# Gates and projections of a gated block, computed with tokens as the stationary operand

## The reference

```python
def hybrid_layer(x, norm_g, w_in, q_norm_g, k_norm_g, sgu_norm_g, w_s, b_s, w_proj_a, w_proj_b, w_out):
    h = rms_norm(x, norm_g)
    q, k, v, z_a, u_b, v_b, z_b, g_a, g_b = jnp.split(h @ w_in, cuts, axis=-1)   # 7 x 1024, 2 x 2048
    ...
    att = moba_attention(q, k, v)                       # 8 heads, 256 tokens: plain causal softmax
    y_a = (att * jax.nn.silu(z_a)) @ w_proj_a           # 1024 -> 2048
    sgu = spatial_gating(jax.nn.gelu(u_b), jax.nn.gelu(v_b), sgu_norm_g, w_s, b_s)
    y_b = (sgu * jax.nn.silu(z_b)) @ w_proj_b           # 1024 -> 2048
    merged = jax.nn.sigmoid(g_a) * y_a + jax.nn.sigmoid(g_b) * y_b
    return x + merged @ w_out
```

## Time and profile before

| | us |
|---|---|
| median of 3 runs | 1817.54 (1817.28 to 1817.78) |
| profiled execution | 1817.34 |
| its span, first to last instruction | 1815.6 |
| TensorE busy | 1805.1 (99%) |
| VectorE busy | 1164.2 (64%) |
| ScalarE busy | 825.0 (45%) |
| weights | 624 transfers of 512 KB |

### The profile page before, as it was taken

The page is one execution under the profiler, slowest core; times in us unless marked ns, Lnnn a source line. Parts: engine busy times, 40 slices in busy tenths (PEclk is TensorE's granted clock), DMA queues, the critical chain, the costliest instruction groups (busy, mean ns, idle before and its releaser), DMA issues.

```text
span 1815.6 us, 28929 instructions
## 1 busy us (share of the span) xinstructions
PE 1805.1 (99%) x9540; PEld 1547.3 (85%) x9540; DVE 1164.2 (64%) x1521; ACT 825.0 (45%) x1116; POOL 129.0 (7%) x163
## 2 busy tenths in 40 slices
PE   9999999999999999999999999999999999999999
PEld 7888888878888888888888887888899888888987
DVE  5457777556755665576456656755687766668844
ACT  6334444446443443344334445744444454444542
POOL 1012323000000000000000000100013010100000
PEclk9999999999999999999999999999999999999999
DMA  7565555555566556556655565565565555555554
GB/s 252 190 222 165 163 169 162 182 177 185 180 218 194 179 187 199 187 185 192 192 192 184 188 194 178 190 204 194 179 192 173 185 175 170 167 171 185 185 190 158
DMA packets 93618, 337.50 MB, mean 186 GB/s; under 512 B 10864, under 2 KB 11008, under 8 KB 93184
## 3 DMA queue, kind: packets, MB, share of 16 engines
q1 hardware_dynamic: 92096, 331.39, 56.6%
q0 software_dynamic: 752, 5.26, 0.8%
q10 hardware_dynamic: 720, 0.17, 0.0%
HBM read 334.67 MB, written 2.11 MB: 185 GB/s over the span
## 4 chain that ended last, share of the span: by engine, by line
PE 98%; DVE 1%; DMA 0%; ACT 0%; POOL 0%; issue 0%; DVEq 0%; ACTq 0%
PE bank L404 43%; PE bank L365 30%; PE bank L367 15%; PE bank L378 5%; PE bank L420 2%; PE bank L533 1%; PE bank L548 1%; PE bank L539 0%; PE bank L532 0%; PE bank L549 0%; DMA res<-in_x 0%; PE bank L487 0%; DVE w_lo L1156 0%; DVE h_both L1169 0%; PE bank L458 0%; PE bank L558 0%
## 5 line engine op out<-in xcount | busy, mean ns | idle before, releaser
L1156 DVE TENSOR_TENSOR w_lo<-raw,w_hi 128x1024 fp32r<-128x1024 f32 x620 | 758.0, 1228 | 432.8 <-ACT w_hi L761 429.4
L761 ACT ACTIVATE w_hi<-raw 128x1024 fp32r<-128x1024 f32 x620 | 655.1, 1058 | 652.3 <-PE bank L404 389.8
L365 PE MATMUL bank<-h_both,w_hi 128*128 128x512 f32 x2176 | 774.9, 400 | 0.0
L367 PE MATMUL bank<-h_both,w_lo 128*128 128x256 f32 x2176 | 609.3, 280 | 0.0
L365 PEld LDWEIGHTS bank<-h_both,w_hi 128*128 128x128 f32 x2176 | 408.8, 188 | 98.1
L367 PEld LDWEIGHTS bank<-h_both,w_lo 128*128 128x128 f32 x2176 | 410.6, 189 | 0.8
L404 PE MATMUL bank<-w_hi,a_both 128*128 128x512 f32 x1216 | 375.0, 390 | 0.0
L404 PE MATMUL bank<-w_hi,h_both 128*128 128x512 f32 x1088 | 336.9, 391 | 0.4 <-DVE w_lo L1210 0.4
L404 PEld LDWEIGHTS bank<-w_hi,a_both 128*128 128x128 f32 x1216 | 227.7, 188 | 47.1
L404 PEld LDWEIGHTS bank<-w_hi,h_both 128*128 128x128 f32 x1088 | 202.8, 188 | 42.1 <-issue 0.8
L404 PE MATMUL bank<-w_lo,a_both 128*128 128x512 f32 x608 | 236.6, 389 | 0.0
(11 more groups left out here) (195 smaller groups left out, 1180.4 us busy)
## 6 DMA issues: line engine op xcount, KB each, us to landing
raw<-in_stream SPq DMA_DIRECT2D x624, 512.0 KB, 3.5
res<-in_x SPq DMA_DIRECT2D x4, 512.0 KB, 8.3
rowg<-in_norm_rows POOLq DMA_DIRECT2D x2, 1024.0 KB, 7.3
gate<-cum_rows POOLq DMA_DIRECT2D x1, 2048.0 KB, 8.7
out<-wide SPq DMA_DIRECT2D x8, 256.0 KB, 4.8
gate<-in_w_spatial POOLq DMA_DIRECT2D x1, 512.0 KB, 5.1
gate<-in_b_spatial POOLq DMA_DIRECT2D x1, 512.0 KB, 6.0
wide<-in_fox_w_f ACTq DMA_DIRECT2D x1, 128.0 KB, 6.7
```

The costliest lines, as they stand in the source:

```text
L365: pe.matmul(dst[:, :], w_hi[:, slot, w], x_both[:, k0 + k, :], start=first and k == 0, stop=False)
L367: mm = pe.matmul(dst[:, 0:TOK], w_lo[:, slot, w], x_both[:, k0 + k, 0:TOK], start=False, stop=last and k == 7)
L761: nc.scalar.activation(w_hi[:, slot, :], raw[:, slot, :], ACT.Copy).then_inc(hi_ready, 1)
L1156: nc.vector.tensor_tensor(w_lo[:, slot, :], raw[:, slot, :], w_hi[:, slot, :].bitcast(F32), ALU.subtract).then_inc(lo_ready, 1)
```

## The change

- z_b's tiles take the form of halves, as u_b and z_a.
- The gates are computed with tokens stationary, as groups of 512 features (8 chunks) into the bank pairs 0/1 and 2/3 in turn; one group goes with each attention head, and the small steps of attention keep their places among the chunks. ScalarE takes tanh straight from the banks, with half the token's norm as its scale (`half_rstd`, a column of a value for each token), so that VectorE neither adds nor scales. `gate` has tokens on the partitions.
- A new pair of semaphores `gate_taken` tells TensorE that a pair is free. VectorE raises both once behind the end of z_a, ScalarE after each gate group, VectorE after each group of the projections. Ahead of the gates TensorE waits for both tile banks and the group pair 0, ahead of the last matrix for `gate_taken[1]`.
- Both projections are groups of 4 chunks, in the same pairs of banks. VectorE multiplies them by the gates and adds, 512 features at a time.
- The merged tensor has tokens on the partitions, so TensorE turns it by 8 transposes for each group (`turn_merged`), through banks 6 and 7; ScalarE and VectorE make the high and low parts from there.
- The host lays out the gates' and projections' weights for groups.

The diff's core (removed lines of the rewritten functions are left out; they are in the listing above):

```diff
-        gate = sb("gate", [P, 32, TOK])
+        gate = sb("gate", [P, NT, 2 * D])
...
+        half_rstd = mean_sq
...
-        merge_b = wide[:, 0:KT * TOK].rearrange("p (k t) -> p k t", k=KT)
+        merge_b = wide[:, 0:NT * D].rearrange("p (t n) -> p t n", t=NT)
...
-        merge_t = [spare[:, b * 256:(b + 1) * 256] for b in range(2)]
-        merge_s = [spare[:, 512 + b * 256:768 + b * 256] for b in range(2)]
+        merged = [spare[:, b * 1024:(b + 1) * 1024].rearrange("p (t n) -> p t n", t=NT) for b in range(2)]
...
+        gate_bank = [bank[0:2], bank[2:4]]
...
+            def group_chunk(c, slot, j, dst, x_hi, x_lo, chunks=GROUP_CHUNKS, k0=0):
 
                 pe.wait_ge(lo_ready, c + 1)
-                last = j == GROUP_CHUNKS - 1
+                last = j == chunks - 1
...
-                                 i + (TILES_BEFORE["sgu_uz"] // 2 + 4), b, halves=False)
+                                 i + (TILES_BEFORE["sgu_uz"] // 2 + 4), b)
...
+            def gate_head(h, b, taken, first):
                 c = FIRST["gates"] + h * 8
                 n = h + FOX_HEADS
+                pe.wait_ge(gate_taken[b], taken)
+                for j in range(GROUP_CHUNKS):
+                    group_chunk(c + j, j % RING, j, gate_bank[b], h_hi, h_lo)
+                    if j == 1:
+                        if not first:
+                            weigh_values(n - 1)
+                        pe.wait_ge(qk_norm_ready, h * 2 + 2)
+                        for q in range(4):
+                            mm = pe.transpose(turned[:, q * P:(q + 1) * P], qk_norm[:, q, :], ident[:, :])
+                        mm.then_inc(qk_turned, 1)
+                    if j == 3:
+                        scores(n)
                 turn_probs(n)
+            for b in range(2):
+                pe.wait_ge(tile_taken[b], TILES_BEFORE["gates"] // 2 + 1)
+            pe.wait_ge(group_taken[0], 18)
+            gate_head(0, 0, 1, True)
+            gate_head(1, 1, 1, False)
+            with pe.Fori(1, MOBA_HEADS // 2) as i:
+                for b in range(2):
+                    gate_head(i * 2 + b, b, i + 1, False)
+            def turn_merged(n):
+                pe.wait_ge(merged_f, 2 * n + 2)
+                if n >= 1:
+                    pe.wait_ge(merged_ready, 4 * n)
+                for b in range(2):
+                    for q in range(2):
+                        for t in range(NT):
+                            f0 = (2 * b + q) * P
+                            mm = pe.transpose(bank[6 + b][:, q * TOK + t * P:q * TOK + (t + 1) * P],
+                                              merged[n % 2][:, t, f0:f0 + P], ident[:, :])
+                    mm.then_inc(merged_turned, 1)
+            def project(name, n, taken, k0, after={}):
+                pe.wait_ge(gate_taken[n % 2], taken)
+                for j in range(4):
+                    group_chunk(FIRST[name] + 4 * n + j, j, j, gate_bank[n % 2], a_hi, a_lo, 4, k0)
+                    if j in after:
+                        after[j]()
             pe.wait_ge(sgu_ready, 8)
+            for n in range(4):
+                project("proj_b", n, 5 + n // 2, 8,
+                        {1: lambda: weigh_values(FOX_HEADS + MOBA_HEADS - 1)} if n == 0 else {})
             pe.wait_ge(att_ready, FOX_HEADS + MOBA_HEADS)
+            for n in range(4):
+                project("proj_a", n, 7 + n // 2, 0, {2: lambda m=n - 1: turn_merged(m)} if n else {})
             def merged_in(j):
                 return lambda: pe.wait_ge(merged_ready, 2 * j + 2)
+            pe.wait_ge(gate_taken[1], 9)
+            group_pair(FIRST["out"], 17, h_hi, h_lo, before={j: merged_in(j) for j in range(8)},
+                       after={2: lambda: turn_merged(3)})
...
+            def gate_head(h, b, first):
                 n = h + FOX_HEADS
+                c = FIRST["gates"] + h * 8
+                lap = h * 2 + (FIRST["gates"] // RING + 1)
+                splits(c, lap, range(2))
                 act.wait_ge(qk_turned, h + 1)
                 nc.scalar.activation(q_head[:, :], turned[:, 0:TOK], ACT.Copy,
                                      scale=hscale[:, 0:1]).then_inc(q_ready, 1)
                 if not first:
                     moba_att_hi(n - 1)
+                splits(c, lap, range(2, RING))
+                split(c + 4, 0, lap + 1)
+                exps(n)
+                for j in range(1, RING):
+                    split(c + 4 + j, j, lap + 1)
+                for t in range(NT):
+                    nc.scalar.activation(gate[:, t, bass.ds(h * GROUP_COLS, GROUP_COLS)], gate_bank[b][t][:, :],
+                                         ACT.Tanh, scale=half_rstd[:, t:t + 1]).then_inc(gate_ready, 1)
+                act.wait_ge(gate_ready, h * 2 + 2)
+                act.sem_inc(gate_taken[b], 1)
                 keep_probT(n)
             act.wait_ge(scale_made, 2)
+            act.wait_ge(half_rstd_ready, 1)
+            gate_head(0, 0, True)
+            gate_head(1, 1, False)
+            with act.Fori(1, MOBA_HEADS // 2) as i:
+                for b in range(2):
+                    gate_head(i * 2 + b, b, False)
+            def merged_to_hi(n):
+                for b in range(2):
+                    act.wait_ge(merged_turned, 2 * n + b + 1)
+                    for q in range(2):
+                        nc.scalar.activation(h_hi[:, 4 * n + 2 * b + q, :], bank[6 + b][:, q * TOK:(q + 1) * TOK],
+                                             ACT.Copy, scale=0.5).then_inc(merged_hi, 1)
+            c = FIRST["proj_b"]
+            for k in range(16):
+                next_split(c + k)
+                if k == 1:
+                    moba_att_hi(FOX_HEADS + MOBA_HEADS - 1)
+            c = FIRST["proj_a"]
+            for k in range(16):
+                next_split(c + k)
+                if k >= 4 and k % 4 == 2:
+                    merged_to_hi(k // 4 - 1)
             c = FIRST["out"]
             for k in range(32 - RING):
+                next_split(c + k)
+                if k == 2:
+                    merged_to_hi(3)
...
                 n = h + FOX_HEADS
+                c = FIRST["gates"] + h * 8
+                rests(c, range(2))
                 dve.wait_ge(q_ready, n + 1)
                 nc.vector.tensor_scalar(k_head[:, :], turned[:, TOK:2 * TOK], hcols[:, 1:2], None,
                                         ALU.mult).then_inc(k_ready, 1)
                 if not first:
                     moba_gated(n - 1)
+                rests(c, range(2, RING))
                 soften(n, mask)
                 if not first:
                     moba_att_lo(n - 1)
+                rest(c + 4, 0)
+                normalise(n)
+                for j in range(1, RING):
+                    rest(c + 4 + j, j)
             dve.wait_ge(za_ready, 8)
+            for b in range(2):
+                dve.sem_inc(gate_taken[b], 1)
             gate_head(0, True)
             with dve.Fori(1, MOBA_HEADS) as h:
                 gate_head(h, False)
+            dve.wait_ge(v_head_ready, FOX_HEADS + MOBA_HEADS)
+            c = FIRST["proj_b"]
+            for n in range(4):
+                for j in range(4):
+                    next_rest(c + 4 * n + j)
+                    if n == 0 and j == 1:
+                        moba_gated(FOX_HEADS + MOBA_HEADS - 1)
+                    if n == 0 and j == 2:
+                        moba_att_lo(FOX_HEADS + MOBA_HEADS - 1)
+                cols_n = slice(n * GROUP_COLS, (n + 1) * GROUP_COLS)
+                cols_b = slice(D + n * GROUP_COLS, D + (n + 1) * GROUP_COLS)
+                dve.wait_ge(gate_ready, 2 * (4 + n) + 2)
+                for t in range(NT):
+                    nc.vector.scalar_tensor_tensor(out=merge_b[:, t, cols_n], in0=gate[:, t, cols_b], scalar=1.0,
+                                                   in1=gate_bank[n % 2][t][:, :], op0=ALU.add,
+                                                   op1=ALU.mult).then_inc(mb_ready, 1)
+                dve.wait_ge(mb_ready, 2 * n + 2)
+                dve.sem_inc(gate_taken[n % 2], 1)
+            def merged_to_lo(n):
+                for b in range(2):
+                    dve.wait_ge(merged_hi, 4 * n + 2 * b + 2)
+                    for q in range(2):
+                        kt = 4 * n + 2 * b + q
+                        nc.vector.scalar_tensor_tensor(out=h_lo[:, kt, :], in0=bank[6 + b][:, q * TOK:(q + 1) * TOK],
+                                                       scalar=0.5, in1=h_hi[:, kt, :].bitcast(F32), op0=ALU.mult,
+                                                       op1=ALU.subtract).then_inc(merged_ready, 1)
+            c = FIRST["proj_a"]
+            for n in range(4):
+                for j in range(4):
+                    next_rest(c + 4 * n + j)
+                    if n >= 1 and j == 2:
+                        merged_to_lo(n - 1)
+                cols_n = slice(n * GROUP_COLS, (n + 1) * GROUP_COLS)
+                if n >= 2:
```

(33 more changed lines are left out.)

149 lines of the change are left out of this document (15 added, 134 removed).

## The result

| | before | after |
|---|---|---|
| median, us | 1817.62 (1817.21 to 1818.35, 15 executions) | 1820.74 (1819.26 to 1822.39, 15 executions) |
| ratio | | 1.0017 (95% interval 1.0009 to 1.0024) |
| profiled execution, us | 1817.34 | 1819.54 |
| its span, us | 1815.6 | 1817.8 |

The changed kernel is 0.17% slower: within the 0.2% that were called no change, and by the interval on its slow side. Its executions also spread more than twice as wide, and fall into three clusters: 4 at 1819.3 to 1819.6 (granted clock 0.999), 6 at 1820.2 to 1820.9 (0.998) and 5 at 1822.2 to 1822.4 (0.997). The profiled one is of the lowest cluster, 1.2 under the median.

A forecast was written before the change was run, and what follows sets the result against it. The prediction took TensorE's own instructions as the bound. Its terms, -4.7 - 0.8 - 2.5 - 0.8 + 3.7 + 2.9 + 4.0 = +1.8 us, gave a median of 1819.3 us, range 1815.5 to 1823.5.

The forecast's parts named there:

- Rates by form: Gates: 64 chunks go from 2.828 to 2.721 us each, small steps cost slightly more; -4.7 us over 8 heads.
- Rival C: Gates don't gain from the group form: chunks at 2.77 us, gain 1.4 instead of 4.7, time 1822.6; chance 0.05.
- Projections and transposes: Projection b -0.8 us, projection a -2.5; four blocks of eight merged-tensor transposes at 0.93 each, +3.7.
- The first wait: Ahead of the gates, TensorE waits for both tile banks and VectorE's semaphore behind z_a; +2.9 us.
- The hand-over: Ahead of the gates, semaphore raised once the remainder is handed over: 2.9 us; at its end 4.1; without awaiting it 2.5.
- The second wait: Ahead of the last matrix, TensorE waits for VectorE's remainder, two products from the banks and semaphore; +4.0 us.
- z_b and what is ahead of it: z_b takes the halves form, 16 chunks going from 2.875 to 2.828 us each; -0.8 us.
- rival A: Clock falls in one of the gaps, costing 2 to 3 us: 1821.3 to 1822.3, both up to 1825.3; chance 0.20.
- The covers: Edits costed at nothing: VectorE's z_b reductions, tanh before `probT`, alternating banks and the merged block cause no TensorE waits.
- Rival B: Waits ahead of the gates and last matrix are hidden, leaving -5.1 us alone: 1812.4; chance 0.08.

The follow-up runs named there:

- only_first: Changed kernel, but the last matrix starts in banks 4 and 5, so only the wait ahead of the gates remains; 1815.70 us.
- the filled kernels: Changed kernel with TensorE running unused matmuls, or unused transposes, during both waits; 1817.51 us with matmuls, 1817.57 us with transposes.
- flip: Changed kernel with the bank pairs swapped, so gates and later stages start in long-free banks and both waits go; 1810.02 us, 0.9958 of the kernel before.
- early_products: Changed kernel, but at projection a's end VectorE forms the two products and raises the semaphore before the last remainder, shortening the second wait; 1816.68 us.

## Why the prediction was right, and where it was not

The time, 1820.74, lies in the range, and the class "no change" is met; the size isn't: +3.1 where +1.8 was forecast, and it took a rival to get there. The terms of the forecast were right to 0.5 us each but for z_b and for the clock, and that these two errors, of opposite sign, left the sum so near is luck.

- **Rates by form.** A group chunk costs 2.721 in gates and projections as in the last matrix. The small steps cost less than assumed: 23.93 - 8 x 2.721 = 2.16 a head, not 2.23. -5.1 against -4.7. Rival C falls.
- **Projections and transposes.** Met to 0.1 us: 0.88 for eight transposes, 0.90 to 0.92 with the longer chunk behind.
- **The first wait.** 3.3 against 2.9. The hand-over was right (4.1 refuted, and 2.5 too); 0.45 us from the remainder's start to TensorE's, where 0.2 was assumed.
- **The second wait.** 3.6 against 4.0 (the parts named there add up to 4.1). The chain of steps was right; two products back to back took 1.28, not 2 x 0.744.
- **z_b and what is ahead of it.** The step that failed: "16 x (2.875 - 2.828) = -0.8" took 2.828 as the halves' rate, which is one of two paces. z_b gained 1.4 and z_a 1.0 without a change of code; the profiled execution lost 0.5 in the first 11 us, which has nothing to do with the change. The prediction had both paces in hand (2.828 in the gates, 2.773 in projection b) and read them as two stages' rates, without asking why one form has two.
- **The clock.** Given 0.20 as rival A, it is what happened: the mean granted clock is below 1.000 in all of the changed kernel's executions, its profile has the fall behind the second wait, and `only_first` has it behind the first; the filled kernels show it, with 3.2 us at the median where 2 to 3 a fall was estimated. The forecast "no fall" was wrong, and came out near by luck, because of gains that were not foreseen, 1.1 us up to the end of z_a and 0.4 in the gates. Without the clock the kernel would stand at 1817.5, level with the one before.
- **The covers.** All held: VectorE in z_b, `probT` behind the tanh, the banks in turn, the merged block. TensorE has no wait in the second block but the two.
- **Rival B** is not what the changed kernel did. But it is what `flip` does, and its price of 1812.4 was 2.4 too high for the reasons above.

## What to carry to other kernels

When a stage changes its form on TensorE, look first at which banks it starts in: a pair that the stage ahead of it fills last cost a drain of 3.3 and 3.6 us here, and the pair that has been free costs a change of an index. Idle times of TensorE like these are to be counted with the slow work behind them, here 3.2 us for the two, and a spread in the times whose clusters follow the mean granted clock is the sign of it. A rate that is read off one stage is the rate of that stage in that execution: compare two stages of the same form before it is multiplied by a count, and ask why they differ.

## What the runs showed of the hardware that was not expected

- The clock fell behind an idle time of 3.3 us as behind one of 3.7, in some executions for longer than in others (0.50 over the whole of 1440 to 1444 in `only_first`, 3.7 us in the changed kernel's profile), in some not at all (1.00 behind the first wait in the profiles of the changed kernel and of `early_products`), and never while idle transposes or matmuls filled the gap (1.000 in all 22 executions).
- The feature-stationary pair of a 512- and a 256-column matmul has two paces, 0.347 and 0.353 us, and keeps the one it starts a stretch with; a single transpose of 0.11 us ahead of each of four stretches left three of them at the faster one (1807.7 against `flip`'s 1810.0), four transposes none (1812.1). Within z_b the same step left five of seven tiles at the faster pace and two at the slower.
